# One step more between the up weights and the down weights in the queue that loads a gated feed-forward stage

## The reference

```
def swiglu(hn, w1, w3, w2):
    return (jax.nn.silu(hn @ w1) * (hn @ w3)) @ w2
h = h + swiglu(rms_norm_2(h, norm_ffn[layer]), ev_ffn_w1[j], ev_ffn_w3[j], ev_ffn_w2[j])
```

## Time and profile before

| | |
|---|---|
| median of 3 runs | 2896.46 us (2895.86 to 2897.5) |
| time of the profiled execution | 2896.46 us |
| its span, first to last instruction | 2894.7 us |
| mean granted TensorE clock | 0.989 of full speed |
| PE busy | 2808.1 us, 97% of the span |
| PEld busy | 2082.2 us, 72% |
| DVE busy | 971.6 us, 34% |
| ACT busy | 390.3 us, 13% |
| HBM read | 613.64 MB |
| chain that ended last | PE 91%, DVE 5%, DMA 2%, ACT 1%, issue 1% |

### The profile page before, as it was taken

One profiled execution on the slowest core, in us unless ns is written; L12 is line 12 of the kernel. 1 busy time (PEld: TensorE's weight loads), 2 busy tenths in 40 slices (PEclk: granted clock), 3 DMA queues, 4 the chain that ended last, 5 costly groups with the idle time before them and its releaser, 6 DMA issues.

```text
span 2894.7 us, 37871 instructions
## 1 busy us (share of the span) xinstructions
PE 2808.1 (97%) x16440; PEld 2082.2 (72%) x16440; DVE 971.6 (34%) x1730; ACT 390.3 (13%) x786; POOL 90.8 (3%) x130
## 2 busy tenths in 40 slices
PE   8999999999999999999999999979999999999998
PEld 6689875776688867677767786567776776676765
DVE  2554112776355312377465663220001001101001
ACT  2220211101212111100141112200000000000000
POOL 0011200000001210000000000000000000000000
PEclk9999999999999999999999999989999999999999
DMA  6231342543333234344324433359999999999995
GB/s 234 95 146 73 139 153 95 203 175 132 124 124 117 99 135 145 147 164 170 141 99 160 175 147 116 124 218 386 372 364 358 378 364 364 382 354 363 385 380 231
DMA packets 56891, 617.19 MB, mean 213 GB/s; under 512 B 6544, under 2 KB 6800, under 8 KB 8720
## 3 DMA queue, kind: packets, MB, share of 16 engines
q1 hardware_dynamic: 54576, 603.27, 54.2%
q0 software_dynamic: 2144, 11.45, 1.0%
HBM read 613.64 MB, written 1.05 MB: 212 GB/s over the span
## 4 chain that ended last, share of the span: by engine, by line
PE 91%; DVE 5%; DMA 2%; ACT 1%; issue 1%; DVEq 0%; SPq 0%; ACTq 0%
PE ps L710 15%; PE ps L1475 14%; PE ps L1162 10%; PE ps L1038 8%; PE ps L1174 7%; PE ps L1485 7%; PE ps L1495 6%; PE ps L1018 4%; PE ps L1515 3%; PE ps L1050 2%; PE ps L691 1%; PE ps L753 1%; PE ps L1140 1%; PE ps L1182 1%; PE ps L1356 1%; PE ps L953 1%
## 5 line engine op out<-in xcount | busy, mean ns | idle before, releaser
L1475 PEld LDWEIGHTS ps<-work,slabA 128*128 128x128 f32 x3584 | 404.4, 192 | 45.2 <-issue 45.2
L1475 PE MATMUL ps<-work,slabA 128*128 128x128 f32 x3584 | 415.0, 277 | 0.9 <-issue 0.9
L1038 PE MATMUL ps<-hT,slabA 128*128 128x256 f32 x1024 | 232.0, 380 | 1.1 <-ACT work L1734 1.1
L710 PE MATMUL ps<-hT,slabA 128*128 128x256 f32 x992 | 220.9, 383 | 2.1 <-DMA slabA<-in_ev_w_in 1.2
L1038 PEld LDWEIGHTS ps<-hT,slabA 128*128 128x128 f32 x1024 | 192.2, 190 | 28.3 <-ACT work L1734 1.9
L710 PEld LDWEIGHTS ps<-hT,slabA 128*128 128x128 f32 x992 | 188.9, 192 | 29.2 <-DMA slabA<-in_ev_w_in 1.4
L1485 PE MATMUL ps<-fbT,work 128*64 128x256 f32 x1792 | 207.4, 384 | 2.0 <-DMA fbT<-in_od_exp_w 2.0
L1495 PE MATMUL ps<-slabB,work 128*128 128x512 f32 x448 | 202.0, 594 | 0.0
L2783 DVE TENSOR_TENSOR work<-work,ps 128x256 f32<-128x256 f32 x56 | 23.6, 421 | 489.4 <-ACT work L1975 489.4
L1485 PEld LDWEIGHTS ps<-fbT,work 128*64 128x64 f32 x1792 | 124.3, 138 | 86.6 <-issue 27.3
L1162 PEld LDWEIGHTS ps<-work 128*128 128x128 f32 x1152 | 139.5, 192 | 21.5 <-issue 21.0
(11 more groups left out here) (391 smaller groups left out, 3071.9 us busy)
## 6 DMA issues: line engine op xcount, KB each, us to landing
slabA<-in_od_exp_w SPq DMA_DIRECT2D x56, 2048.0 KB, 9.7
fbT<-in_od_exp_w SPq DMA_DIRECT2D x56, 2048.0 KB, 10.0
slabB<-in_od_exp_w SPq DMA_DIRECT2D x56, 1024.0 KB, 8.5
fbT<-in_od_exp_w SPq DMA_DIRECT2D x56, 1024.0 KB, 10.8
slabA<-in_w_in SPq DMA_DIRECT2D x24, 2048.0 KB, 7.8
slabA<-in_mlp_w SPq DMA_DIRECT2D x16, 2048.0 KB, 9.3
slabB<-in_mlp_w SPq DMA_DIRECT2D x32, 1024.0 KB, 4.7
slabA<-in_ev_ffn_w SPq DMA_DIRECT2D x11, 2048.0 KB, 7.6
```

Source lines behind the costliest of these rows:

```text
L710: last = mm(ps[0:rows, g % PROJ, c0:c0 + n], lhs(k), rhs(k), start=(k == 0), stop=(k == KD - 1))
L1038: last = mm(ps[:, b, 0:T], side["gates"][:, k, c % 4 * P:(c % 4 + 1) * P], hT[:, k, :], start=(k == 0), stop=(k == KD - 1))
L1475: last = mm(ps[:, 0, (2 * w + j) * P:(2 * w + j + 1) * P], v[:, k, j * P:(j + 1) * P], xs[:, k, :], start=(k == 0), stop=(k == KD - 1))
```

## The change

The loop that orders the loads runs one turn longer for the gated stage, and each down slab is written one turn later: B(i) stood behind A(i+1), and stands behind A(i+2).

```
             def ffn_steps(steps, gated, w13, w2, last=None):
 
-                for n in range(steps + 1):
+                for n in range(steps + 1 + gated):
                     if n < steps and gated:
                         ringA.load(sp, [(whole, w13[n])], ("hidden_psum", 2) if n < plain_steps(gated) else ("up_products", 4))
                     elif n < steps and n % 2 == 0:
                         ringA.load(sp, [(whole, w13[n // 2])], ("hidden_psum", 4) if n < plain_steps(gated) else ("up_products", 4))
-                    if n:
-                        ringB.load(sp, [(whole, w2[n - 1])], last if n == steps else None)
+                    if n > gated:
+                        i = n - 1 - gated
+                        ringB.load(sp, [(whole, w2[i])], last if i == steps - 1 else None)
```

## The result

| | before | after |
|---|---|---|
| median of four runs each | 2896.98 us (2895.86 to 2897.73) | 3030.76 us (3025.83 to 3031.96) |
| time and span of the profiled execution | 2896.46, 2894.7 us | 3032.99, 3031.2 us |
| mean granted clock | 0.989 | 0.968 |

The changed kernel takes 133.8 us more; the ratio is 1.0459 with an interval of 1.0441 to 1.0477. The page first: span, busy time of each engine, and each engine's share of the chain that ended last.

What follows compares the result with a forecast made beforehand. TensorE, busy 97% of the span, was taken to bound the kernel. Eight turns' waits 106.5, the first wait 10.1 and the clock 23.4 make 140 us on 2896.46: 3036.5 us, range 3012 to 3056.

Steps and rivals of the forecast that it cites:

- the landing: Down slab B(i) behind up slab A(i+2): down 11.07 us after the issue of A(i+2).
- TensorE bounds, and a wait lengthens the program: Gated stage: TensorE busy 150.90 of 150.90 us, so every microsecond it is made to wait lengthens the program.
- Which wait comes up: VectorE waits for each late down slab, 10.1 us at B(0), 15.5 at the others; TensorE waits nine times on line 2162.
- The growth per turn, 13.3 us: Wait from issue of A(i+2) to first down piece grows from 4.51 to 17.82 us; eight turns, 106.5 us.
- Anew in each step: The wait comes anew each step, as the next pair is issued only after the up product behind it; turn 32.2 us.
- The clock, 9 x 2.6 = 23.4 us: TensorE's clock falls to half in each of nine stalls, losing 2.6 us each time, 23.4 us.
- The end of the stage, the up slabs: nothing: B(9) at the stage's end costs nothing; earlier up slabs gain nothing, having 3.9 us of room already.
- The clock recovers at once: Rival: clock recovers at once or falls only in the first wait; 116.6 to 119.2 us more, 3013 to 3016; chance 0.05.
- low all the way: Rival: TensorE's clock stays low throughout, 129 us in the place of 23.4; 3142 us; chance 0.04.
- B lands sooner: Rival: down slab overtakes the up slab, landing 5.07 us in the place of 11.07; 2983 us; chance 0.03.
- paid once: Rival: pipeline takes up the delay at B(0), then runs at its old turn; 10.1 + 2.6, 2909 us; chance 0.01.
- Not slower: Rival: up slab no longer stands behind B(i-2)'s wait; at best TensorE's 1.8 us wait goes, 2894.7 us; chance 0.02.

Runs made afterwards that it cites:

- one late slab: Only B(0) goes out late, behind A(2); the other down slabs as in the kernel before: 2903.93 us, +8.8, ratio 1.0030.
- the run with four: B(0) to B(3) go out late, behind the up slab two steps on; B(4) and later as in the kernel before: 2951.65 us, ratio 1.0189.
- the held slabs: Kernel before with B(1) to B(8) held until two, three or all four parts of up(i) are done, still ahead of A(i+2): 2894.54, 2925.98, 2968.60 us.
- the run with twelve fillings: Changed kernel with 12 products of a zero matrix on TensorE ahead of every first down piece: 3018.37 us, ratio 1.0427.
- its second run: The changed kernel timed once more, unaltered, on the chip of the run with 12 zero-matrix products: 3029.23 us, ratio 1.0467.
- 24, 12 and 14 fillings: Changed kernel with 24, 12 or 14 zero-matrix products ahead of every first down piece: 3080.62, 3018.37 and 3011.07 us.
- two parts: Kernel before with B(1) to B(8) held until the second of four parts of up(i) has ended: 2894.54 us, ratio 1.0003.
- The kernel before with `hidden` first: Kernel before with hidden values and hidden sums ahead of the down sums on VectorE, loads as before: 2929.33 us, ratio 1.0110.

## Why the prediction was right

Forecast were 3036.5 us (3012 to 3056) and slower; measured 3030.76. Of the 140 us forecast the account finds 132.3: the landing was put 8.2 us too high, the clock 0.5 too low. By its steps:

- *TensorE bounds, and a wait lengthens the program.* Right: VectorE is as busy as before, the program behind the stage takes the same time, and the account closes.
- *Which wait comes up.* Right: nine of VectorE for the slab, 9.4 us at B(0) (10.1 forecast) and 14.4 to 15.0 at the others (15.5), and nine of TensorE on line 2162, now 2163.
- *The growth per turn, 13.3 us.* It was 12.38, and 99.0 for 106.5. The term that was off is the landing. I took 10.7 and 10.2 us from pairs in the kernel before; here it is 9.6 at the median, behind an issue 0.38 us after A's: 10.0 in the place of 11.07. Why it is shorter stays open (see the last section). VectorE's terms came out as taken. The first wait is 0.7 us less than forecast, for a shorter landing too.
- *Anew in each step.* Right, as one late slab (+8.8), four (+56.5) and nine (+133.8) show.
- *The clock, 9 x 2.6 = 23.4 us.* Right in sum, 23.9, and with the place named: the fall behind each wait. That the size fits so closely is in part luck. It was read from one gap elsewhere; the other row at hand gave 3.0, and the size isn't one number here: 1.84 us in the first turn, 2.43 to 2.91 in the next seven, 2.94 behind the last. The Trainium skill (*TensorE: Matmul & The Clock Gate*, section on HAM oscillation) says that such a loop pays on every tile and not once; the trace agrees, with nine returns and 23.9 us.
- *The end of the stage, the up slabs: nothing.* Right: the stage's end behind the last clock return is as long as before, and TensorE waits for no transfer.

The rivals fell each by a row. "The clock recovers at once" (3013 to 3016) by the 3.75 us pieces; "low all the way" (3142) by the stretch from 1581.50 at 1.00; "B lands sooner" (2983) by 9.47 us of landing, and the run in which B really goes ahead of A shows how such a landing looks, 4.8 us and 2968.6; "paid once" (2909) by the run with four. "Not slower" by the waits; the held slabs show where its point lies: a down slab issued 9.7 us ahead of A(i+2) (1592.10 to 1601.78) costs nothing, 4.4 us ahead of it 31 us, just ahead of it 73 (eight slabs each), and behind it 134 (nine slabs).

No version beat the kernel before. The 1.8 us of its one wait would be too little to tell from no change, and weren't tried for.

## What to carry to other kernels

Before a load is moved back, compare three times of one turn: its issue, its landing behind whatever stands before it in its queue, and the moment its reader is ready. The time between landing and reader is the room. Beyond it every microsecond is paid in every turn, if the next issue depends on work that stands behind the wait. Follow the path from the landing through all that stands behind the waiting instruction in its stream, here 6.8 us of VectorE's work. And add to each new wait of TensorE the return of its clock: 1.8 to 2.9 us here behind waits of 11 to 13 us, and on average still a little over 1 us behind waits of 2.7 to 3.3 us.

## What the runs showed of the hardware

- *Short waits cost the clock too.* Waits of 2.3 to 3.5 us in each turn let it fall in most turns, not in all (first pieces of 1.95 to 3.65 us for the same four products). The length alone does not decide: behind a wait of 2.32 us the first piece took 2.55 us, behind one of 3.09 us 1.95, both in the run with twelve fillings. Waits of up to 1.8 us ahead of a first down piece never did.
- *The landing isn't one number.* Issued 0.38 us behind an up slab, a down slab landed after 9.6 us at the median where TensorE stood idle meanwhile (the changed kernel; 9.8 in its second run) and after 10.2, 10.7 and 10.6 where it was kept at work (24, 12 and 14 fillings). The cause wasn't tested. Held slabs with nothing ahead of them landed after 4.8 us at the median while TensorE was fully busy (two parts), so work on TensorE alone does not slow every landing. The kernel before with `hidden` first, whose TensorE rests for 2.9 us a turn, doesn't fit either end: 9.6 at a distance of 0.86 us, where the kernel before has 10.2.
- *The order in the queue decides who lands first.* At the median 1 MB issued 0.4 us behind 2 MB landed after 9.6 us, and 0.4 us ahead of it after 4.8. The 2 MB then landed after 9.2 us where they take 7.6 in front.
